# Output-gate and mixer output projections in groups of 1024 columns with seven block products in some units

## What is computed

```python
def token_mixer(h, w_in, ..., gla_norm_g, w_proj_a, w_proj_b, w_out):
    z = h @ w_in
    z_sg, q, k, v, og, g_lr, m_a, m_b = jnp.split(z, idx, axis=-1)
    ...
    o = gla_chunked(q, k, v, log_a)                      # four heads of 512 value columns
    o = rmsnorm(o, gla_norm_g) * jax.nn.silu(og)         # og: h @ 2048 columns of w_in
    y_b = o.reshape(B, S, GLA_DV)
    merged = sigmoid(m_a) * (y_a @ w_proj_a) + sigmoid(m_b) * (y_b @ w_proj_b)
    return merged @ w_out

x = x + rmsnorm(token_mixer(rmsnorm(x, ...)), post_norm_mix)
h = rmsnorm(x, ...)                                      # input of the cross-attention
```

## Time and profile before

| | us |
|---|---|
| median of three runs | 2054.79 |
| span of the profiled execution | 2053.1 |
| TensorE busy | 2044.2 (100%) |
| VectorE busy | 1524.8 (74%) |
| ScalarE busy | 988.5 (48%) |
| granted TensorE clock, mean | 1.000 |
| DMA: share of 16 engines on SyncE's queue | 56.1% |

### The profile page before, as it was taken

How to read it: one execution, slowest core, us unless ns; L and a number is a source line. 1 busy time by engine, 2 the same in 40 slices (tenths; PEclk the granted TensorE clock), 3 DMA queues, 4 the chain that set the end, 5 groups by cost and what they waited for, 6 DMA issues and landing times.

```text
span 2053.1 us, 26543 instructions
## 1 busy us (share of the span) xinstructions
PE 2044.2 (100%) x10788; PEld 1757.5 (86%) x10788; DVE 1524.8 (74%) x1857; ACT 988.5 (48%) x986; POOL 16.0 (1%) x34
## 2 busy tenths in 40 slices
PE   9999999999999999999999999999999999999999
PEld 7888888888888888888888888888888888888987
DVE  5776786554656767678988887888886768987776
ACT  6443363454444455555554544445454434454642
POOL 0000000000000000000000000000000000000000
PEclk9999999999999999999999999999999999999999
DMA  9766656546566765555656565555566654554462
GB/s 328 220 191 194 193 167 213 180 153 210 152 198 226 259 233 185 184 186 174 209 191 200 189 202 188 194 189 192 198 212 236 185 174 144 186 184 144 144 244 105
DMA packets 298346, 397.99 MB, mean 194 GB/s; under 512 B 18945, under 2 KB 223793, under 8 KB 296561
## 3 DMA queue, kind: packets, MB, share of 16 engines
q1 hardware_dynamic: 294096, 375.28, 56.1%
q0 software_dynamic: 3408, 18.92, 2.5%
q10 hardware_dynamic: 720, 2.11, 0.3%
HBM read 392.09 MB, written 4.19 MB: 193 GB/s over the span
## 4 chain that ended last, share of the span: by engine, by line
PE 97%; DVE 1%; DMA 1%; ACT 1%; issue 0%; SPq 0%; DVEq 0%; ACTq 0%
PE ps L723 91%; PE pm L723 5%; PE pm L726 1%; DVE wl L1884 0%; DMA raw<-in_w_in 0%; DMA xin<-in_x_by_features 0%; DVE cv L1892 0%; ACT wh L1298 0%; ACT xt L1298 0%; DVE yA L1884 0%; DVE up L2066 0%; ACT cv L1298 0%; DVE up L1884 0%; ACT L1298 0%; DVE xt L1892 0%
## 5 line engine op out<-in xcount | busy, mean ns | idle before, releaser
L1884 DVE TENSOR_TENSOR wl<-raw,wh 128x2048 fp32r<-128x2048 f32 (+2 forms) x368 | 790.0, 2161 | 284.0 <-ACT wh L1298 211.6
L1298 ACT ACTIVATE wh<-raw 128x2048 fp32r<-128x2048 f32 (+1 forms) x357 | 664.1, 1873 | 318.6 <-PE ps L723 268.4
L723 PE MATMUL ps<-xt,wh 128*128 128x512 f32 (+2 forms) x2736 | 638.4, 389 | 0.2 <-ACT wh L1298 0.2
L723 PEld LDWEIGHTS ps<-xt,wh 128*128 128x128 f32 (+1 forms) x2736 | 505.0, 188 | 101.7 <-issue 0.7
L723 PE MATMUL ps<-wh,xt 128*128 128x512 f32 x1600 | 387.1, 391 | 1.8 <-ACT wh L1298 1.8
L723 PEld LDWEIGHTS ps<-wh,xt 128*128 128x128 f32 x1600 | 298.1, 188 | 64.5 <-issue 1.6
L723 PEld LDWEIGHTS ps<-xt,wl 128*128 128x128 f32 x2704 | 336.3, 192 | 7.0
L723 PE MATMUL ps<-xt,wl 128*128 128x256 f32 x2704 | 338.6, 283 | 0.0
L723 PE MATMUL ps<-wl,xt 128*128 128x512 f32 x800 | 203.0, 390 | 0.4 <-DVE wl L1884 0.4
L723 PEld LDWEIGHTS ps<-wl,xt 128*128 128x128 f32 x800 | 149.9, 188 | 32.7 <-DVE wl L1884 1.7
L1298 ACT ACTIVATE cv<-up,vt 128x256 f32<-128x256 f32 x88 | 52.5, 601 | 220.3 <-DVE up L1884 220.3
(11 more groups left out here) (405 smaller groups left out, 1601.5 us busy)
## 6 DMA issues: line engine op xcount, KB each, us to landing
raw<-in_w_in SPq DMA_DIRECT2D x146, 1024.0 KB, 5.3
raw<-in_ffn_w_up SPq DMA_DIRECT2D x84, 1024.0 KB, 5.2
raw<-in_ffn_w_down SPq DMA_DIRECT2D x43, 1024.0 KB, 5.1
raw<-in_w_out SPq DMA_DIRECT2D x32, 1024.0 KB, 5.3
raw<-in_w_proj_b SPq DMA_DIRECT2D x16, 1024.0 KB, 5.4
raw<-in_w_proj_a SPq DMA_DIRECT2D x8, 1024.0 KB, 5.4
raw<-in_xa_wk SPq DMA_DIRECT2D x4, 1024.0 KB, 5.4
raw<-in_xa_wq SPq DMA_DIRECT2D x4, 1024.0 KB, 5.3
```

Source lines behind the costliest of these rows:

```text
L723: return p.matmul(out, l, r, start=start, stop=stop, skip_group_check=share)
L1298: return a.activation(out, in_, func, bias=bias, scale=scale)
L1884: return v.tensor_tensor(out, a, b, op)
```

## The change

`og` becomes two wide groups of eight units, with seven block products in units 3 and 5 of `og0` and 1, 3 and 5 of `og1`; `wo` becomes two wide groups with seven block products in units 2 and 5 of each. That is five and four units. The functions for wide groups take their operands, forms and places from the group instead of from `ac` alone.

New work: `h1_forms` three times (beside `ma5`, `ma6`, `ma7`), `mg_forms` in `evac_pb` of `pb2` and `pb5`, `dif_lo` and `dif_hi` for nine units, `og0_sums`, `og1_sums`, `wo0_sums`, `wo1_sums`, and the evacuation of the wide groups by adding into `og` and `yA` in SBUF. The silu of `og` and the squares of `wo` are then taken from SBUF, and the gain is multiplied in SBUF.

Moved: `gla_out0` and `1` both at `og0`'s first unit, `2` and `3` at its second; `gla_rstd` to the middle of `og0`; the gates later, two of them into `mb0`; `mem_spread` from `wo0`'s third unit to its first; the `mem_split` steps from `wo1` into `wo0`; `junk_o` to another place. The scratch that is kept for the descriptors of GpSimd's DMAs becomes 4096 bytes in each partition, and the forms lie in the space that this frees, below `BASE` (`LOW`). The loads of `og` and `wo` weights have rows of 1024 columns (4 KB) instead of 512.

```diff
--- before.py
+++ after.py
+SCRATCH = 4096
 BASE = 16512
+LOW = (SCRATCH + 128 - BASE) // KB
...
         add("v%d" % i, w_in, KC, [(4096 + 512 * i, 512)], "tok", "h1")
-    for i in range(4):
-        add("og%d" % i, w_in, KC, [(6144 + 512 * i, 512)], "tok", "h1")
+    for i in range(2):
+        add("og%d" % i, w_in, KC, [(6144 + 1024 * i, 1024)], "wide", "h1", chunk=2, seven=PAIRS["h1"][1 - i:])
     for i in range(8):
         add("mb%d" % i, w_in, KC, [(10256 + 256 * i, 256)], "feat", "h1", chunk=8)
     for i in range(8):
         add("pb%d" % i, I["w_proj_b"][0], KC, [(256 * i, 256)], "feat", "yb", chunk=8)
-    for i in range(4):
-        add("wo%d" % i, I["w_out"][0], KC, [(512 * i, 512)], "tok", "mg")
+    for i in range(2):
+        add("wo%d" % i, I["w_out"][0], KC, [(1024 * i, 1024)], "wide", "mg", chunk=2, seven=PAIRS["mg"])
     for i in range(2):
...
-    ("ma1", 0): ["sg_mix"], ("ma4", 0): ["gate_zero"], ("pa2", 0): ["gate_w"], ("q0", 0): ["gate_g"],
+    ("ma1", 0): ["sg_mix"], ("ma5", 0): ["h1_forms0"], ("ma6", 0): ["h1_forms1"], ("ma7", 0): ["h1_forms2"], ("ma4", 0): ["gate_zero"], ("pa2", 0): ["gate_w"], ("q0", 0): ["gate_g"],
     ("q0", 0.5): ["gate2_0"], ("q0", 1): ["gate2_1"], ("q0", 1.5): ["gate2_2"], ("q1", 0): ["gate2_3", "gate_log"],
     ("q2", 0): ["gate_la"], ("q2", 1): ["gate_scan"], ("q3", 0): ["gate_spans012"], ("q3", 1): ["gate_spans3", "gate_exp"],
     ("k0", 0): ["gate_exp_spans0"], ("k0", 1): ["gate_q"], ("k1", 0): ["gate_exp_spans4"],
     ("v0", 1): ["gate_k12"], ("v0", 3): ["gate_k3"],
     ("v1", 2): ["gla_scores0"], ("v2", 0): ["gla_scores2"],
-    ("og0", 0): ["gla_out0"], ("og0", 1): ["gla_out1"], ("og0", 2): ["gla_out2"], ("og0", 3): ["gla_out3"],
-    ("og1", 0): ["gla_rstd"], ("og1", 2): ["gla_gate0"], ("og2", 2): ["gla_gate1"], ("og3", 2): ["gla_gate2"],
-    ("mb0", 1): ["gla_gate3"],
+    ("og0", 0): ["gla_out0", "gla_out1"], ("og0", 1): ["gla_out2", "gla_out3"], ("og0", 6): ["og0_sums"],
+    ("og0", 4.5): ["gla_rstd"], ("og1", 2): ["gla_gate0"], ("og1", 4): ["gla_gate1"], ("og1", 6): ["og1_sums"],
+    ("mb0", 0): ["gla_gate2"], ("mb0", 1): ["gla_gate3"],
     ("mb2", 0): ["gla_turn0"], ("mb2", 1): ["gla_turn4"], ("mb3", 0): ["gla_turn8"], ("mb3", 1): ["gla_turn12"],
-    ("pb4", 0): ["mem_sums"], ("pb6", 0): ["mem_scale"], ("wo0", 2): ["mem_spread"],
-    ("wo1", 0): ["mem_split0"], ("wo1", 1): ["mem_split4"], ("wo1", 2): ["mem_split8"], ("wo1", 3): ["mem_split12"],
+    ("pb4", 0): ["mem_sums"], ("pb6", 0): ["mem_scale"], ("wo0", 0): ["mem_spread"],
+    ("wo0", 2.5): ["mem_split0"], ("wo0", 3): ["mem_split4"], ("wo0", 5.5): ["mem_split8"], ("wo0", 6): ["wo0_sums", "mem_split12"],
+    ("wo1", 6): ["wo1_sums"],
...
+PAIRS = {"h1": (1, 3, 5), "mg": (2, 5), "ac": SEVEN}
...
+    at_dif = {"wo0": ((G + 8, G + 12), (B, B + 4)), "og0": ((A, A + 4), (A + 8, A + 12)), "dw00": ((B, B + 4), (C + 16, M + 12)), "dw10": ((XT, XT + 4), (XT + 8, XT + 12))}
+    dif, dif_l = [{g: [tile("%s_%s%d" % (name, g, q), kb, [128, 1024], dt) for q, kb in enumerate(at[0])]
+                   for g, at in at_dif.items()} for name, dt in (("dif", F), ("dif_l", R))]
+    dif_h = {g: [tile("dif_h_%s%d" % (g, q), kb, [128, 1024], R) for q, kb in enumerate(at[1])] for g, at in at_dif.items()}
+    for its in (dif, dif_l, dif_h):
+        its["dw01"], its["og1"], its["wo1"] = its["dw00"], its["og0"], its["wo0"]
...
+        def h1_forms(i):
+            heard()
+            to_v.add(act(h1_form_h[:, 4 * i:4 * i + 4, :], v3(x_form[i], 128), ACT.Copy))
...
             to_v.add(act(xth[:, 2 * i:2 * i + 2, :], v3(mt[i % 2], 256), ACT.Copy))
+            if i in PAIRS["mg"]:
+                j = PAIRS["mg"].index(i)
+                heard()
+                to_v.add(act(mg_form_h[:, 4 * j:4 * j + 4, :], v3(mg_form[j], 128), ACT.Copy))
...
-        def evac_wo(i, blocks):
-            name = "wo%d" % i
-            for tb in blocks:
-                filled(name, tb)
-                j = tb * 4 + i
-                square("junk_wo", junk_wo, ps[set_of[name]][tb], cell("part1", 8)[:, j:j + 1])
+        def evac_wo(i):
+            for tb in range(2):
+                for n in range(2):
+                    a.wait_ge(*evacuated("wo%d" % i, 2 * tb + n))
+                j = tb * 2 + i
+                square("junk_m", junk_m, yA[:, tb, 1024 * i:1024 * i + 1024], cell("part1", 4)[:, j:j + 1])
...
+        def evac_og(name, tb):
+
+            step(last[name])
+            filled(name, tb)
+            for n in range(2):
+                c = 1024 * int(name[2]) + 512 * n
+                o = og[:, tb, c:c + 512]
+                tt(o, bank(name, 2 * tb + n), o, ALU.add).then_inc(evacuated(name, 2 * tb + n)[0], 1)
+            if tb:
+                last["silu_" + name] = [from_act.tick() for _ in range(4)][3]
+
+        def h1_forms(i):
+
+            k = 2 * PAIRS["h1"][i]
+            a11, a21, a12, a22 = [x_sum[:, 128 * q:128 * q + 128] for q in range(4)]
+            s1, s2, s3, s4 = [x_form[i][:, 128 * q:128 * q + 128] for q in range(4)]
+            v.wait_ge(s_h1, KC)
+            step(own.add(tt(v3(x_sum, 256), xth[:, k:k + 2, :].bitcast(F), xtl[:, k:k + 2, :].bitcast(F), ALU.add)))
+            tt(s1, a21, a22, ALU.add)
+            step(own.add(tt(s3, a21, a11, ALU.subtract)))
+            step(own.add(tt(s2, s3, a22, ALU.add)))
+            to_act.add(tt(s4, a12, s2, ALU.subtract))
+            heard()
+            lo_part(h1_form_l[:, 4 * i:4 * i + 4, :], v3(x_form[i], 128), h1_form_h[:, 4 * i:4 * i + 4, :]).then_inc(s_form["h1"], 1)
...
             lo_part(xtl[:, c, :], v3(m_, 256), xth[:, c, :]).then_inc(s_mg, 1)
+            if i in PAIRS["mg"]:
+                mg_forms(i, m_)
+
+        def mg_forms(i, m_):
+
+            j = PAIRS["mg"].index(i)
+            a11, a21, a12, a22 = [m_[:, 128 * q:128 * q + 128] for q in range(4)]
+            s1, s2, s3, s4 = [mg_form[j][:, 128 * q:128 * q + 128] for q in range(4)]
+            tt(s1, a21, a22, ALU.add)
+            step(own.add(tt(s3, a21, a11, ALU.subtract)))
+            step(own.add(tt(s2, s3, a22, ALU.add)))
+            to_act.add(tt(s4, a12, s2, ALU.subtract))
+            heard()
+            lo_part(mg_form_l[:, 4 * j:4 * j + 4, :], v3(mg_form[j], 128), mg_form_h[:, 4 * j:4 * j + 4, :]).then_inc(
+                s_form["mg"], 1)
...
-        def evac_wo(i, blocks):
-            name = "wo%d" % i
-            c = slice(512 * i, 512 * i + 512)
-            v.wait_ge(s_gb1, 16)
-            v.wait_ge(s_used, after("pb7"))
-            for tb in blocks:
-                filled(name, tb)
-                heard()
-                tt(yA[:, tb, c], ps[set_of[name]][tb], gb[:, c], ALU.mult).then_inc(s_accfree[set_of[name]], 1)
+        def evac_wo(name, tb):
+
+            i = int(name[2])
+            step(last[name])
+            filled(name, tb)
+            for n in range(2):
+                o = yA[:, tb, 1024 * i + 512 * n:1024 * i + 512 * n + 512]
+                tt(o, bank(name, 2 * tb + n), o, ALU.add).then_inc(evacuated(name, 2 * tb + n)[0], 1)
+            if tb:
+                c = slice(1024 * i, 1024 * i + 1024)
+                v.wait_ge(s_gb1, 16)
+                for b in range(2):
+                    heard()
+                    tt(yA[:, b, c], yA[:, b, c], gb[:, c], ALU.mult).then_inc(s_gain, 1)
...
-            v.wait_ge(*evacuated("wo2"))
-            v.wait_ge(*evacuated("wo3"))
             ssq = cell("ssq1", 2)
-            t = own.add(v.tensor_reduce(ssq, v3(cell("part1", 8), 4), AX.X, ALU.add))
+            t = own.add(v.tensor_reduce(ssq, v3(cell("part1", 4), 2), AX.X, ALU.add))
             step(t)
             r = rstd("p1", ssq, D, EPS, 2)
             step(last["p1"])
+            v.wait_ge(s_gain, 4)
...
             if u.g.kind == "wide" and u.last:
-                evac_dw(u.g.name, 0)
+                evac_wide(u.g.name, 0)
             if u.n + 2 < NU and not moved_low(u.n + 2):
...
-    nc = bacc.Bacc("TRN2", target_bir_lowering=False, num_devices=1)
+    nc = bacc.Bacc("TRN2", target_bir_lowering=False, num_devices=1, dynamic_dma_scratch_size=SCRATCH)
```

More of the change, by code:

```diff
@@ L159, in groups_of @@
         for i in range(2 - half):
-            add("dw%d%d" % (half, i), down, HF, [(1024 * i, 1024)], "wide", "ac", chunk=2, k_off=half * HF)
+            add("dw%d%d" % (half, i), down, HF, [(1024 * i, 1024)], "wide", "ac", chunk=2, k_off=half * HF, seven=SEVEN)
         for i in range(2, 4) if half else ():
@@ L379, in build @@
     junkB = tile("junkB", B, [128, D])
-    junk_wo = tile("junk_wo", B + 4, [128, 512])
+    mg_form = [tile("mg_form%d" % j, B + 4 + 2 * j, [128, 512]) for j in range(len(PAIRS["mg"]))]
+    mg_form_h = tile("mg_form_h", LOW, [128, 4 * len(PAIRS["mg"]), 128], R)
+    mg_form_l = tile("mg_form_l", LOW + 6, [128, 4 * len(PAIRS["mg"]), 128], R)
     junk_xo = tile("junk_xo", A, [128, 512])
@@ L449, in build @@
     bst = tile("bst", B, [128, 2, 48])
```

(23 more changed lines are left out.)

113 lines of the change are left out of this document (66 added, 47 removed).

## The result

| | before | after |
|---|---|---|
| median of seven runs | 2054.61 us (2054.30 to 2055.03) | 2060.80 us (2060.07 to 2061.62) |
| profiled execution, span | 2053.1 us | 2059.1 us |
| mean granted clock | 1.000 | 0.998 |

The ratio is 1.0028, with an interval of 1.0019 to 1.0038: slower by 0.3%. I had forecast 2056.8 and no difference that can be told; the range ended at 2060.0. The time lies outside it, on the slow side, 4.0 us above the forecast.

The account below looks back on a forecast made before the run. TensorE, busy for the whole span, was taken as the bound. Products saved (-6.1 us) and waits of 0.2 at og1, 5.2 entering wo0, 1.4 at wo1 and 1.3 behind it gave +2.0: 2056.8 us, range 2050.6 to 2060.0.

Parts of the forecast that it names:

- What is removed: In og and wo, nine units lose three products each: 27 x 0.227 = 6.1 us, all on the path.
- The entry to `wo0`: At wo0's start TensorE waits 5.2 us, in three pieces, for VectorE to empty pb7's banks; forms and a load delay it.
- the sum: Whole kernel: -6.1 + 0.2 + 5.2 + 1.4 + 1.3 = +2.0 us, so 2056.8 in the runs; chance 0.42.
- the rule that each microsecond above 7.4 counts in full: Load of wo0's second unit: up to 7.4 us nothing changes; above it each microsecond adds in full.
- rival (C): At wo0's entry the second unit's load lands late beside mem_in: 2058.6 at 9.2 us, 2060 with another late; chance 0.16.
- The sentence drawn from the Trainium skill: At wo0's entry: DMA engines alternate between queues packet by packet, so doubling w_out's rows raises its share against GpSimd's queue.
- The pair that I called an agreement: Load times beside GpSimd's loads: 9.2 us with 2 KB rows, 6.7 with 4 KB, taken as agreeing in kind.
- Through `wo0`: VectorE is the later engine, needing 43.5 us against TensorE's 42.2, so TensorE waits 1.4 us at wo1 instead of 0.7.
- Behind `wo1`: At the transposes of yA the chain shifts 2.55 us; the fourth bank is 1.3 ahead, leaving 1.3 us of waiting.
- (B): The chain before wo0 absorbs the forms, so the entry costs 1.6 us: 2052.5 in all; chance 0.28.
- (D): Nothing waits anywhere, the other stages' cover holds: -6.1 us, so 2048.7; chance 0.11.
- (E): A seven unit of og or wo is no shorter, its operands late each time: 2062.9; chance 0.03.

Follow-up runs that it names:

- the load alone: Changed kernel with the four mem_in loads held back until the high part of wo0's second unit is made: 2059.13 us.
- the output gate alone: Changed kernel with only og in 1024-column groups; wo stays in 512-column groups without forms or sums: 2051.58 us, ratio 0.9984 to the kernel before.
- The fill products: Changed kernel with 22 extra products of 512 columns, results unused, put where TensorE pauses at wo0's start: 2059.52 us.
- The swap: Changed kernel with VectorE's low part of the next group's second unit ahead of emptying block 0 at every wide group's end: 2060.68 us.
- the kernel without a pause: Changed kernel with VectorE's two reductions that empty pb7's banks ahead of both low parts of wo0: 2055.58 us, ratio 1.0003 to the kernel before.
- the pause of 1.7: Changed kernel with the two reductions that empty pb7's banks between the low parts of wo0's first and second unit: 2058.32 us.
- the ten with 3.1: Changed kernel with wo0 and wo1 still in 1024-column groups but of plain units only, no forms of mg, no sums: 2058.92 us.

## Why the prediction was wrong

- **What is removed**: right, 27 x 0.227; `og` alone gave 3.2 (five units, less 0.2 at `og1`, as forecast), a seven unit of `wo` takes 4.76 (716.45 to 721.21), and `ma`, `og` and `mb` had no pause.
- **The entry to `wo0`**: the mechanism was right, the size 2.1 us short: 7.3 where the sum had 5.2. The failed term is the load. I took 6.7 us from another place because its rows were as long, and called 9.2 a rival; but 9.2 was the median of this very load and the next beside these very `mem_in` loads. It took 9.53. By the rule that each microsecond above 7.4 counts in full that would be 2.1; the run with the load alone measured 1.8 and left an entry of 5.5, close to the sum's 5.2. The other 0.3 is as much as the forms delayed the chain beyond the sum's size (3.9 against 3.6). This is rival (C)'s mechanism at its edge. The sentence drawn from the Trainium skill ("DMA: Bandwidth & Descriptors", Queues, rings and completion order) spoke for a shorter load with rows of 4 KB. No run bears it out: with rows of 2 KB the load took 8.8 us in the kernel before and 8.98 in the one with the output gate alone, with rows of 4 KB 9.53. The pair that I called an agreement, 9.2 and 6.7, differs in its neighbours too.
- **What the pause does to the products behind it**: absent from the sum and from every rival, so put at nothing. The clock fell to half and cost 2.2 us at its place. The fill products show that the standing still did it. With the load's 1.8 it is as much as the whole miss of 4.0; the other differences cancel (+0.3 at the entry, -0.75 at `wo1`, +0.2 behind it, +0.3 ahead of `og`). With one of the two taken away the time would have stayed in the range: 2059.52 with the clock held, 2059.13 with the load alone. The Trainium skill ("TensorE: Matmul & The Clock Gate", Part 1: The HAM clock gate) says that the chip sets TensorE's clock by how busy it has been, and halves it after idling; the trace agrees (0.53 behind the pause), and I had priced a pause of 5 us at its length alone.
- **Through `wo0`**: VectorE's 43.5 us was right (43.7 in the run with fill; busy 32.66 of 35.00 us in the changed kernel). The wait at `wo1` was 0.65, not 1.4, since TensorE at half clock was itself late; without the half clock it was 1.47. So the half clock hid a part of its own cost.
- **Behind `wo1`**: 1.5 against 1.3, near by luck in part. The sum had all of it at the banks of the second set, which cost 0.9; 0.5 more came from `yA`, which it didn't count. The swap took away the wait for `yA` and left 0.8 at the banks. They wait for VectorE's eight low parts `xt`, 2.0 us later against TensorE than before; no run moved these.
- The rest is 0.3 us lost ahead of `og`. At 109 us, ahead of every step that a kernel here adds or moves, the profiled executions already stand between -0.4 and +1.3 from before's, so I take it for no effect of the change.
- The cases: (B) and (D) fell with the pause of 5.7, (E) with the seven units at 4.76 us and with the kernel of the output gate alone. (C)'s load came, and with it a cost that no case had.

In sum: -6.1 + 0.2 + 7.3 + 2.2 + 0.65 + 1.5 + 0.3 = +6.05, and the span grew by 6.05.

## What to carry to other kernels

A pause of TensorE is priced at its length plus what the clock takes behind it, 1.6 to 2.9 us in the profiled executions with a pause of 3.1 or more; ask whether the engine that ends the pause can do that step earlier. When a change takes work from the busiest engine and gives some to another, read the other's busy share in that stage with the new work in it. In the kernel before, VectorE had in `wo0` and `wo1` (now `wo0`), and then in `wo2` and `wo3` (now `wo1`):

```profile
698.00:742.00 44.00, 32.69 (x35) 1.00 0.75 258
742.00:786.00 44.00, 21.43 (x13) 1.00 0.69 245
```

That is 74% and 49%; the `memT` parts lay in the first. The weights' differences with their parts and the sums brought the first to 95% (43.78 of 46.00, in the kernel without a pause), so the saving had nowhere to go until `memT` parts were moved into the second. And a duration for a moved transfer is to be taken from that transfer in its own neighbourhood, whatever else is changed about it.

## What was not expected of the hardware

- The granted clock after a pause isn't fixed by the pause. In the profiled executions it fell to half behind pauses that cost 3.1, 3.9, 5.3 (the kernel with the order swapped) and 5.7 us, for 14, some 7, some 7 and 11 products of 512 columns, and not behind one of 1.7. But three of the ten executions with the pause of 1.7 have a mean clock under 1.000, and two of the ten with 3.1 have 1.000.
- The load of `wo0`'s second unit (1 MB) took 5.4 us with `mem_in` held back. Beside the four loads of 512 KB on GpSimd's queue it took 8.8 to 9.0 with rows of 2 KB (kernel before, output gate alone), and 9.1 to 9.6 with rows of 4 KB.
